# A convolution layer in the order of the token tiles, its first weight panel run by halves of the tokens

## What is computed

```python
# end of the first block: h is the residual, two expert rows are added to each token
h = h + hier_moe(n2, ...)
x = rms_norm(h, final_gain)
# convolution layer (D = 1024): modulated norm, four projections, a convolution over three tokens
mod = silu(c) @ w_mod + b_mod                 # shift, scale, gate
n = rms_norm_2(x, g, eps) * (1 + scale) + shift
b, cc, xx, z = split(n @ conv_w_in)           # 1024 -> 4 x 1024
t = cc * xx
y = b * (k0 * t[s - 1] + k1 * t[s] + k2 * t[s + 1]) * silu(z)
x = x + gate * (y @ conv_w_out)
```

## Time and profile before

| | |
|---|---|
| median of three runs | 1532.05 us (1529.07 to 1536.29) |
| the profiled execution | 1529.32 us, of which the span from first to last instruction is 1527.6 us |
| TensorE, VectorE, ScalarE busy | 92%, 46%, 32% of the span |
| mean granted clock of TensorE | 0.976 of full speed |

### The profile page before, as it was taken

How to read it: one execution, slowest core, us unless ns; L and a number is a source line. 1 busy time by engine, 2 the same in 40 slices (tenths; PEclk the granted TensorE clock), 3 DMA queues, 4 the chain that set the end, 5 groups by cost and what they waited for, 6 DMA issues and landing times.

```text
span 1527.6 us, 17831 instructions
## 1 busy us (share of the span) xinstructions
PE 1406.1 (92%) x6818; PEld 973.4 (64%) x6818; DVE 702.0 (46%) x1282; ACT 486.6 (32%) x727; POOL 39.5 (3%) x73
## 2 busy tenths in 40 slices
PE   6999995899988888999739999999999999999997
PEld 5877774444433343343217888778888888888886
DVE  4478647321110111010067656456255666666555
ACT  6462435001100010111054222325344444444552
POOL 2000000000000000000020010000000000000000
PEclk9999898899999999999969999999999999999999
DMA  9827335399999997899986553212312112212201
GB/s 358 345 107 275 115 138 220 144 426 427 427 424 429 424 428 318 360 427 424 428 292 265 217 210 123 81 56 85 111 56 107 59 56 87 79 56 81 86 15 56
DMA packets 36806, 336.80 MB, mean 220 GB/s; under 512 B 4560, under 2 KB 4688, under 8 KB 18384
## 3 DMA queue, kind: packets, MB, share of 16 engines
q1 hardware_dynamic: 29632, 304.69, 49.3%
q0 software_dynamic: 6624, 29.89, 5.5%
q10 hardware_dynamic: 432, 0.60, 0.1%
HBM read 312.62 MB, written 22.54 MB: 219 GB/s over the span
## 4 chain that ended last, share of the span: by engine, by line
PE 47%; DMA 2%; DVE 1%; ACT 1%; issue 0%; POOL 0%; SPq 0%; POOLq 0%; ACTq 0%; PEld 0%; PEldq 0%; DVEq 0%
PE ps L335 46%; DMA ring<-in_wts_dram 2%; PE ps L814 1%; DVE hres L1935 0%; DMA ar<-y_scratch,rt 0%; POOL ar L2270 0%; DVE ar L1943 0%; PE ps L777 0%; DVE ar L2046 0%; DMA y_scratch<-gate 0%; PE ps L341 0%; DVE hres L2049 0%; DVE ar L2193 0%; ACT ar L983 0%; ACT b_NH L1249 0%
## 5 line engine op out<-in xcount | busy, mean ns | idle before, releaser
L335 PE MATMUL ps<-ar 128*64 128x512 f32 (+5 forms) x814 | 172.1, 487 | 25.4 <-issue 7.5
L335 PE MATMUL ps<-ring,ar 128*64 128x512 f32 x784 | 178.3, 600 | 16.5 <-DMA ring<-in_wts_dram 8.3
L1814 DVE TENSOR_TENSOR ar<-ar,ps 128x256 f32<-128x256 f32 x34 | 14.3, 421 | 371.2 <-ACT ar L1125 368.7
L335 PE MATMUL ps<-b_NH,b_WH 128*128 128x512 f32 x688 | 178.0, 397 | 0.8 <-ACT b_NH L989 0.8
L335 PE MATMUL ps<-b_NH,b_WL 128*128 128x512 f32 x688 | 172.4, 389 | 0.0
L335 PE MATMUL ps<-b_NL,b_WH 128*128 128x512 f32 x688 | 170.1, 389 | 0.0
L1385 DVE TENSOR_TENSOR b_WL<-ring,b_WH 128x1024 fp32r<-128x1024 f32 x106 | 129.5, 1221 | 73.9 <-ACT b_WH L935 73.9
L935 ACT ACTIVATE b_WH<-ring 128x1024 fp32r<-128x1024 f32 x106 | 112.1, 1058 | 123.2 <-PE ps L335 122.3
L335 PEld LDWEIGHTS ps<-ar 128*64 128x64 f32 (+3 forms) x814 | 79.5, 162 | 110.1 <-issue 91.8
L335 PEld LDWEIGHTS ps<-b_NH,b_WL 128*128 128x128 f32 x688 | 129.2, 188 | 27.1
L335 PEld LDWEIGHTS ps<-b_NL,b_WH 128*128 128x128 f32 x688 | 129.1, 188 | 26.8
(11 more groups left out here) (306 smaller groups left out, 1900.6 us busy)
## 6 DMA issues: line engine op xcount, KB each, us to landing
ring<-in_wts_dram SPq DMA_DIRECT2D x83, 2048.0 KB, 16.9
ar<-in_wts_dram SPq DMA_DIRECT2D x25, 2048.0 KB, 27.9
spare<-in_wts_dram SPq DMA_DIRECT2D x24, 2048.0 KB, 27.0
ring<-in_wmod_dram SPq DMA_DIRECT2D x24, 512.0 KB, 4.8
ar<-in_wmod_dram POOLq DMA_DIRECT2D x24, 512.0 KB, 4.0
y_scratch<-gate POOLq DMA_DIRECT2D x11, 1024.0 KB, 21.2
y_scratch<-gate SPq DMA_DIRECT2D x44, 128.0 KB, 26.5
y_scratch<-ar SPq DMA_DIRECT2D x24, 128.0 KB, 24.5
```

The lines of the kernel that those rows point to most:

```text
L335: return pe.matmul(o, l, m, start=start, stop=stop, skip_group_check=True)
L1814: return dve.tensor_tensor(h.rearrange("p (a c) -> p a c", a=2), g_.rearrange("p (a c) -> p a c", a=2), ps[:, b, :].rearrange("p (a g c) - ...
```

## The change

The convolution layer keeps the tokens in the order of the token tiles. `TT` gets 768 columns in place of 514 and two buffers in place of four: the product is written to columns 128 to 639, and the last tile's and the first tile's parts a second time, shifted by one, on either side, so that the neighbour of a token is 128 columns away. The strided accesses of the shift and of `yTc` go.

The first panel runs by two halves of the tokens (tiles 0 and 1, then 2 and 3), for all four of its feature tiles. `turn_half`, `lead_half` and `shift_half` of the next layer are made general. Half 0 is transposed to banks 4 to 7, shifted and split, and used while ScalarE and VectorE still work on tiles 2 and 3; these are transposed before the last feature tile's WH x NL of half 0. All four weight chunks of `P_C0` have to be there at the start, so `hi` and `lo` of chunks 2 and 3 move ahead of the adds and go to a buffer `w4` of their own, which lies over one ring slot; SyncE's load of `P_C0 + 3` into this slot, and the loads behind it, wait until the first panel is done. ScalarE and VectorE have a new order: tile 0 is carried to its scaling before tile 1 is squared, and half 0 is shifted before the last gather is added. The modulation steps begin one panel later, GpSimd's loads for them wait for `N_CV + 16`.

```diff
+W4 = {cno(P_C0, j): j - 2 for j in (2, 3)}
+S_W4 = 2
...
-    return c - 4 if c - 2 in W2 else c - 2
+    return c - 4 if c - 2 in W2 or c - 2 in W4 else c - 2
...
+        if S_W4:
+            sb("ring_below", [128, S_W4 * 4096])
+        w4 = [sb("w4" + n, [128, 2, 1024], F32R) for n in "hl"]
+        if S_W4 < RING - 1:
+            sb("ring_above", [128, (RING - 1 - S_W4) * 4096])
...
-        Cc, TT, CV = area(4096, 4, 512), area(6144, 4, 514), area(8200, 4, 512)
-        tmpx = [area(14344, 512), area(14856, 512)]
+        Cc, TT, CV = area(4096, 4, 512), area(6144, 2, 768), area(8200, 4, 512)
         tmpc = [area(5632, 512), area(16640, 512)]
-        tmph = [area(4096 + 256 * j, 256) for j in range(6)]
+        tmph = [[area(o + 256 * j, 256) for j in range(6)] for o in (14344, 4096)]
...
+            b = (((4, 5, 6, 7), (4, 5, 6, 7)), ((2, 3, 4, 5), (6, 7, 2, 3)))[l][hf][k // 2]
...
+            def turn_half(l, hf, x, un):
+                for p in (2 * hf, 2 * hf + 1):
+                    pe.wait_ge(s_un[p], un)
+                    for k in range(8):
+                        t = pe.transpose(half_bank(l, hf, k)[:, (p % 2) * 128:(p % 2) * 128 + 128],
+                                         x[:, p, k * 128:(k + 1) * 128], ident[:, :])
+                        if p % 2:
+                            t.then_inc(S["turn"], 1)
+
+            def lead_half(i, ops, nb, hf, banks, between=None):
+
+                NH, NL, WH, WL = ops
+                o = slice(256 * hf, 256 * hf + 256)
+                for k in range(8):
+                    pe.wait_ge(S["nh"], nb + 8 * hf + k + 1)
+                    for j, b in enumerate(banks):
+                        c = cno(i, j)
+                        h, lo = chunk_dst(WH, c, True), chunk_dst(WL, c, True)
+                        if k == 0 and not hf:
+                            pe.wait_ge(S["lo"], c + 1)
+                        mm(ps[:, b, o], h[:, k, :], NH[:, k, o], k == 0, False)
+                        mm(ps[:, b, o], lo[:, k, :], NH[:, k, o], False, False)
+                for j, b in enumerate(banks):
+                    h = chunk_dst(WH, cno(i, j), True)
+                    if j == 3 and between:
+                        between()
+                    for k in range(8):
+                        if j == 0:
+                            pe.wait_ge(S["nl"], nb + 8 * hf + k + 1)
+                        t = mm(ps[:, b, o], h[:, k, :], NL[:, k, o], False, k == 7)
+                    if hf:
+                        t.then_inc(S["wdone"], 1)
 
...
-            turn(x0c, U_PK + 9, banks_of(T_CV))
+            turn_half(0, 0, x0c, U_PK + 9)
+            lead_half(P_C0, op_b, N_CV, 0, (0, 1, 2, 3), lambda: turn_half(0, 1, x0c, U_PK + 9))
+            lead_half(P_C0, op_b, N_CV, 1, (0, 1, 2, 3))
...
-                    lead_panel(i, op_b, N_CV, (0, 1, 2, 3), [(S["ttd"], 1), (S["tta"], 1)])
-                    run(feature_tiles(i, op_b, (0, 1, 2, 3), (2, 3), lambda j: None))
-                else:
+                if c:
...
-                if c in (33, 34):
+                if c in (33, 34, 35, 36):
...
-            def turned_shift(ops, l, natural, tb, nb, tmps):
+            def shift_half(l, hf, ready):
+                nb, tb, xb = (N_CV, N_DL)[l] + 8 * hf, (T_CV, T_DL)[l] + 8 * hf, 8 * l + 4 * hf
+                tmps = tmph[l]
+
                 def shifted(k):
-                    o, src = tmps[k % 4], ps[:, k, :]
-                    if natural:
-                        o, src = o.rearrange("d (i p) -> d p i", p=4), src.rearrange("d (p i) -> d p i", p=4)
-                    act.wait_ge(S["turn"], tb + k + 1)
-                    if k >= 4:
-                        act.wait_ge(S["nl"], nb + k - 3)
-                    act.activation(o, src, ACT.Identity, scale=mcol[:, l, 0, k:k + 1],
+                    act.wait_ge(S["turn"], tb + k // 2 * 2 + 2)
+                    if hf or k >= 6:
+                        act.wait_ge(S["nl"], nb + max(k - 5, 0))
+                    act.activation(tmps[k % 6], half_bank(l, hf, k), ACT.Identity, scale=mcol[:, l, 0, k:k + 1],
                                    bias=mcol[:, l, 1, k:k + 1]).then_inc(S["tta"], 1)
 
-                shifted(1)
+                act.wait_ge(S["mpd"], 5 * l + 5)
+                if ready:
+                    act.wait_ge(*ready)
                 for k in range(8):
-                    act.wait_ge(S[("ttd", "tta")[k % 2]], 4 * l + k // 2 + 1)
-                    act.activation(ops[0][:, k, :], tmps[k % 4], ACT.Copy).then_inc(S["nh"], 1)
-                    if k % 2 == 1 and k < 7:
-                        shifted(k + 2)
+                    if k in (0, 1, 4, 5):
+                        shifted(2 + k)
+                    act.wait_ge(S[("ttd", "tta")[k // 2 % 2]], xb + k // 4 * 2 + k % 2 + 1)
+                    act.activation(op_b[0][:, k, 256 * hf:256 * hf + 256], tmps[k % 6], ACT.Copy).then_inc(S["nh"], 1)
...
-            hi(P_C0, 1)
+            for n in range(1, 4):
+                hi(P_C0, n)
...
             pk_squares(0)
-            pk_squares(1)
             pk_root(0, rs2, 6)
             pk_unit(0)
-            pk_squares(2)
+            pk_squares(1)
             pk_root(1, rs2, 6)
             pk_unit(1)
+            pk_squares(2)
+            shift_half(0, 0, (S["fgc"], 1))
             pk_squares(3)
             pk_root(2, rs2, 6)
             pk_unit(2)
             pk_root(3, rs2, 6)
             for p in range(4):
                 pk_root(p, rs, 10)
-
-
-            act.wait_ge(S["mpd"], 5)
-            act.wait_ge(S["fgc"], 1)
-            turned_shift(op_b, 0, True, T_CV, N_CV, tmpx + zz)
+            shift_half(0, 1, None)
...
-                            if j < 2:
-                                hi(i, j + 2)
-                            elif j == 3:
+                            if j == 0:
                                 hi(i + 1, 0)
...
-            def turned_shift(ops, l, natural, tb, nb, tmps):
+            def shift_half(l, hf):
+                nb, tb = (N_CV, N_DL)[l] + 8 * hf, (T_CV, T_DL)[l] + 8 * hf
+                tmps = tmph[l]
+
                 def shifted(k):
-                    o, src = tmps[k % 4], ps[:, k, :]
-                    if natural:
-                        o, src = o.rearrange("d (i p) -> d p i", p=4), src.rearrange("d (p i) -> d p i", p=4)
-                    dve.wait_ge(S["turn"], tb + k + 1)
-                    if k >= 4:
-                        dve.wait_ge(S["nl"], nb + k - 3)
-                    dve.tensor_scalar(o, src, mcol[:, l, 0, k:k + 1], mcol[:, l, 1, k:k + 1], ALU.mult,
-                                      ALU.add).then_inc(S["ttd"], 1)
+                    dve.wait_ge(S["turn"], tb + k // 2 * 2 + 2)
+                    if hf and k < 2:
+                        dve.wait_ge(S["nl"], nb)
+                    dve.tensor_scalar(tmps[k % 6], half_bank(l, hf, k), mcol[:, l, 0, k:k + 1], mcol[:, l, 1, k:k + 1],
+                                      ALU.mult, ALU.add).then_inc(S["ttd"], 1)
 
                 shifted(0)
+                shifted(1)
                 for k in range(8):
-                    if k % 2 == 0 and k < 6:
-                        shifted(k + 2)
                     dve.wait_ge(S["nh"], nb + k + 1)
-                    dve.tensor_tensor(ops[1][:, k, :], tmps[k % 4], f32(ops[0][:, k, :]),
+                    o = slice(256 * hf, 256 * hf + 256)
+                    dve.tensor_tensor(op_b[1][:, k, o], tmps[k % 6], f32(op_b[0][:, k, o]),
                                       ALU.subtract).then_inc(S["nl"], 1)
+                    if k < 2:
+                        shifted(4 + k)
...
-            lo(P_C0, 0)
-            lo(P_C0, 1)
+            for n in range(4):
+                lo(P_C0, n)
...
             pick(1, 0)
-            pick(1, 1)
             dve.wait_ge(S["fgsq"], 1)
             products(0)
+            pick(1, 1)
+            both(0)
             pick(2, 0)
-            both(0)
+            products(1)
+            both(1)
             pick(2, 1)
-            products(1)
             pick(3, 0)
-            both(1)
+            shift_half(0, 0)
             pick(3, 1)
...
-            turned_shift(op_b, 0, True, T_CV, N_CV, tmpx + zz)
+            shift_half(0, 1)
...
-                            dve.tensor_tensor(TT[:, j, 1:513], ps[:, 4 + j, :], Cc[:, j, :], ALU.mult).then_inc(S["xr"], 1)
+                            tt, xp, xc = TT[:, j % 2, :], ps[:, 4 + j, :], Cc[:, j, :]
+                            dve.tensor_tensor(tt[:, 128:640], xp, xc, ALU.mult)
+                            dve.tensor_tensor(tt[:, 1:128], xp[:, 384:511], xc[:, 384:511], ALU.mult)
+                            dve.tensor_tensor(tt[:, 640:767], xp[:, 1:128], xc[:, 1:128], ALU.mult).then_inc(S["xr"], 1)
                             kc = cols[:, C_CK + 3 * t:C_CK + 3 * t + 3]
                             dve.wait_ge(S["xr"], t + 1)
```

(14 more changed lines are left out.)

102 lines of the change are left out of this document (20 added, 82 removed).

## The result

The changed kernel takes 1527.4 us in the median (1526.55 to 1530.34), the kernel before beside it 1532.83 us (1529.07 to 1536.29). The ratio is 0.9967 with a 95% interval of 0.9954 to 0.9980, so 5.1 us are gained, 3.1 to 7.0. That is a third of a percent. The forecast was 1528.8 us, in a range of 1523.5 to 1533.5; it was added up on the 1532.05 us of three runs of the kernel before, where all six have 1532.83.

What follows compares the result with a forecast made beforehand. TensorE's idle hole between 774 and 805 us bounds the kernel. Second panel at 799.0 + 22.4 + 1.9 + 1.5 = 824.8 against 828.14 gains 3.3 us: 1526.0, plus 2.7 for the median, 1528.8 us; range 1523.5 to 1533.5.

Steps and rivals of the forecast that it cites:

- Part 1: Hole before the first panel: two token tiles in place of four put the first matmul at 799.0, 6.3 us earlier.
- Part 2: First panel on TensorE: halves make 192 matmuls of 256 columns, 22.4 us, plus 1.91 us for 16 middle transposes.
- Part 3: First matmuls at low clock: it rises 3.1 us after 799.0, costing 1.5 us, between 0 and 2.6.
- Part 4: Between the panel's halves: tiles 2 and 3 are ready 2 us before TensorE asks at 810.8; no wait.
- Part 5: Remaining edits, to products, loads, modulation and rounding, mostly behind the first panel: hidden, costing nothing.
- (a): Convolution product in three pieces: adds 0.44 us to each VectorE tile, hidden from TensorE.
- (c): SyncE's fourth and fifth panel loads start near 825, still in time for rounding 38 us after the second panel begins.
- (d): GpSimd's modulation loads wait until near 817, not 813; last steps end 22 us later, near 962, for use at 1009.
- A: Rival, first panel: late tiles 2 and 3, late gathers or a late clock thin the gain to 1.2 us; chance 0.20.
- B: Rival, later panels: shifted loads and modulation make a weight chunk wait, giving the gain back, 1532 us; chance 0.06.
- C: Rival, first half: the clock stays low through its main loop, costing 7 us, 1534.3 us; chance 0.06.
- D: Rival, hole: VectorE's extra chunks hold back the adds, first matmul stays near 804, 0.2 us lost, 1532.2; chance 0.08.

Runs made afterwards that it cites:

- e5: Changed kernel with 150 idle transposes ahead of tile 0 and 22 between tiles 0 and 1, keeping TensorE busy; 1526.77 us, ratio 0.9968.
- e6: Kernel before with only the new layout: token order, product in three pieces, unstrided full-width shift, no halves; 1531.18 us, ratio 0.9998.
- e1: Kernel before run once more with no edit; 1531.41 us, ratio 0.9998.
- e7: Changed kernel with VectorE's main convolution product cut in 16 pieces of 32 columns; one profiled execution, rest of span behind the second panel's start 702.80 us.
- e3: Changed kernel with half 0 shifted only after tiles 2 and 3 are scaled, on both engines; 1534.39 us, ratio 1.0032.
- e10: e5 with one VectorE add moved ahead of tile 1's products and one behind the shift of half 0; 1526.76 us, ratio 0.9972.

## Why the prediction came out as it did

**Part 1, right.** Products of tile 0 were expected 1.27 us earlier and came 1.06 earlier (790.05 is 15.14 us behind the last copy; 789.87 of the earlier trace rows is 16.20). The first matmul was expected 6.3 us earlier and came 6.15 earlier. The extra chunks on VectorE ate its waits for gathers, as walked through: the adds at 785.98 have no bracket, where those of before waited 0.67 us at 785.60.

**Part 2, right in kind, 0.3 short.** At full clock the panel takes 24.56 us (e5), where 22.4 + 1.9 = 24.3 was the sum. The matmuls of a group of 16 near the end start 0.119 us apart (821.90 to 823.81), not 0.117. A gap of 2.5 ns, as the Trainium skill (TensorE: Matmul & The Clock Gate, Part 1) has it, would by estimate give 0.3 us less than the sum. The rows don't agree with that: 256 columns at 2.4 GHz are 0.107 us, so the gap is about 12 ns. The 0.26 us that the prediction works out from it is 0.24 (96 x 2.5 ns). The 1.0 us of waits for the strided shift were real: they vanish in e6.

**Part 3 is the term that was mis-sized.** I had carried the 3.1 us of the rows of before over to the new start, which gave a rise 3.1 us behind the first matmul, or 1.5 us of cost. The clock rose 1.6 and 1.3 us behind it, a cost of 0.7 to 0.8, and e5 measures 0.6 to 0.7. The larger error stood on the other side of the subtraction. I took the profiled execution of before as its usual one, with the clock up 1.1 us ahead of the first matmul. In e1 it is up 4.2 us behind, and in e6, which has the same block of transposes ahead, 1.7 behind. The timed executions point the same way: the mean granted clock over the whole span was 0.976 in the profiled one, but 0.974 in the median of the 70 of before beside the experiments, of which 11 reach 0.976; in after it was 0.977 in both. The Trainium skill (same page and part) says the number of matmuls before the rise differs between executions of one kernel; the two traces of before agree, 5.3 us apart. I had drawn from it that after would scatter. It is before that did.

**Part 4, right.** Tile 3 was ready at 810.03 for transposes at 811.65: 1.6 us of slack, 2.0 forecast. The second half's first matmul follows the first half's last without a wait; the copy that it needs ends at 814.08 (813.67 + 0.41) and it starts near 814.3, so 0.2 us were to spare, 0.3 forecast.

**The sum.** On the profiles the gain is 3.70 us (54.47 - 50.77), 3.3 forecast; 2.5 us of it show in their times, as the last copy came 1.24 us later in after's execution. The steps themselves were thus off by 0.4 us (the clock +0.7, the rest -0.3). The timed runs have 5.1 us (3.1 to 7.0) and 4.6 (3.2 to 6.0). Two ways of counting over both executions of each kernel lie within both intervals: the mean of the sums gives 55.3 - 50.7 = 4.6 us, the way from the last copy to the end of the span 3.9. So how the 1.3 to 1.8 us beyond the forecast divide between the clock of before and the scatter of the runs isn't shown. That the forecast time is off by only 1.4 us has some luck in it: the gain was about 2 us larger by the medians, while the kernel before came out 0.8 us slower than the three runs it was added up on. In the range, the lower end of its terms is 1526.3 (1528.8 - 1.5 - 1), not 1526.7; nothing hangs on it.

**Part 5, right.** No wait appears behind 825.68 that wasn't there before, and the rest of the span is 699.32 against 699.46 us. (a) added 0.39 us to VectorE's tile, 0.44 forecast (e7 shows how little more would do); the loads and the modulation, (c) and (d), left no trace.

**The rivals.** A fails by its own marks: no wait between the halves, the first matmul 25.5 us behind the last copy, the clock early. B has no row: TensorE waits for no weight chunk. C fails in after, but e3 shows its mechanism: with a pause of 6.8 us ahead of the halves the low clock lasts 5.4 us into them and costs 2.4 (26.98 against 24.56). What was held against C, that the block of 3.48 us of transposes had been enough in before, doesn't hold: in e1 the same block came ahead, 3.67 us long, and the clock stayed low for 4.2 us more. D fails; the extra chunks held back nothing.

**What stays open.** What sets the time of the rise from one execution of before to the next wasn't found. Squaring tile 2 behind the first copies on ScalarE, which would take 1.05 us out of the way to the first matmul, wasn't tried; e10 shows only that this square stands there.

## What to carry to other kernels

A start on half of the data pays as long as the first half has enough work to cover the second half's preparation: with all four feature tiles the timed gain was 4.6 us (e2), with two about half of that. When a start won't move, look at each engine that feeds it: here the adds on VectorE and a square on ScalarE ended within 0.1 us of each other, and taking away one showed the other. Count the cost of narrower matmuls from pairs of starts in the trace. Before a difference of a few microseconds is forecast, look at a second trace of the kernel before: in the two of this kernel the rise of the clock lay 5.3 us apart and the local stretch 1.7 us, beside a change worth 4 to 5 us.
